# Rounded parts for both halves of the experts' down weights, with one subtraction per slot moved to GpSimd

## The chip, the core and the metric

The program runs on one core of one Trainium2 chip. The metric is the device time of one execution in microseconds (us). The core has TensorE (matrix products, PE in the rows; its weight loads are PEld), VectorE (DVE), ScalarE (ACT), GpSimd (POOL) and SyncE (SP, used here for transfers only).

## The reference, cut to what matters

Two transformer layers with attention are followed by two layers of another block. Each of these two ends in a mixture of experts:

```python
def hier_moe(h, w_rg, b_rg, w_re, b_re, w_gate, w_up, w_down):
    ...  # a gate for each of 16 experts; two experts of one group of four get one
    a = jnp.einsum('nd,edf->nef', hf, w_gate)     # d = 1024, f = 256
    b = jnp.einsum('nd,edf->nef', hf, w_up)
    hid = jax.nn.silu(a) * b * gates.astype(h.dtype)[..., None]
    return jnp.einsum('nef,efd->nd', hid, w_down).reshape(shp)
```

Everything is float32. The first mixture has 512 rows, the second 256. The change is in the last product, `hid` by `w_down`, where each expert has a weight of 256 x 1024.

## The kernel before

**Products in parts.** TensorE takes float32 operands at full precision, or operands rounded to a shorter form (fp32r) at a faster pace. For most products the kernel makes of each operand a high part, which is the rounded value, and a low part, which is the rest. It then adds three products: high by high, low by high, high by low. ScalarE makes the high parts (an activation `Copy` into an fp32r tile), VectorE the low parts (`tensor_tensor` with `subtract`, raw minus high).

**Slots.** Routing sorts the rows of a mixture by group of experts into tiles of 128 rows. A tile is worked on by the four experts of its group, one after the other. One expert on one tile is a slot `s`. The first mixture has 7 tiles and 28 slots, the second 5 tiles and 20 slots, 48 in all. Slots from 16 on take their weights by an index (`DMA_INDIRECT`, issued by GpSimd), the others by plain transfers that SyncE issues. A text that says "slot 0 to 3 of a group" means `s % 4`.

**What a slot does** (`moe` in each engine's program):

- TensorE, `gates_and_ups(s)`: 24 products of 128x512, with the transposes of the previous slot's hidden values (`turn_hidden(s - 1)`) after the 13th. Where `s % 4 == 1`, `turn_rows` follows with 8 transposes for the next tile. Then comes `downs(s - 1)`.
- ScalarE: tanh of slot `s` (L1765), in slot 1 of a group `ht_hi` (L1748), the rounding of the gate and up weights of slot `s + 2` (L1463), in slot 0 of a group the copy of a finished tile (L1755), the rounding of half of the down weight of slot `s` (L1458), and two copies of the turned hidden values (L1778, L1779).
- VectorE: two operations that finish the hidden values (L2433, L2436), in slot 1 of a group `ht_lo` (L2420), four subtractions of 128x1024 for gate and up of slot `s + 2` (`gu_lo`, L1981), one for the down weight (`dn_lo`, L1975), and `ut_lo` (L2445).
- GpSimd: gathers of rows (L2645) and of weights by index (L2650), no arithmetic within the slots.

**The down product.** The 256 rows of the weight are two halves of 128. `dn_raw[:, at, 0]` is the first half and is multiplied in full float32 with `ut_all`. `dn_raw[:, at, 1]` is the second half and goes in three products of rounded parts. Buffers for the down weight (`at = s % 2`) are two. The tile's sum over four slots stays in PSUM banks 5 and 6.

**Order.** Each engine has one program written out by hand, and waits stand in it as semaphore values. An instruction that waits holds up everything behind it on its engine. GpSimd's loop over slots first gathers rows where due, then the down weight of `s + 1` by index, then gate and up weights of `s + 4`, each once its buffer is free. The slots that gather gate and up weights are 12 to 23 of the first mixture and 12 to 15 of the second.

Of the kernel before, what the change touches and what calls it, by code (L numbers as in the profile page):

```python
# [7 lines left out]
F32 = mybir.dt.float32  # L8
# [346 lines left out]
def build(nc, a, out):  # L355
    with ExitStack() as ctx:
# [36 lines left out]
        v_tok, _ = sb("v_tok", [P, 1280])  # L393
# [9 lines left out]
        dn_raw, _ = sb("dn_raw", [P, 2, 2, D], F32, offset=acc_at)  # L403
        h_all = [sb("h_all0", [P, DT, S2], F32, offset=big2)[0], sb("h_all1", [P, DT, S], F32, offset=big2)[0]]
# [291 lines left out]
        def tensor_program(e):  # L696
# [416 lines left out]
            def moe(layer):  # L1113
# [100 lines left out]
                def downs(s):  # L1214
                    at_, first, last = s % 2, s % IN_GROUP == 0, s % IN_GROUP == IN_GROUP - 1
                    if first:
                        claim(5)
                        claim(6)
                    e.wait_ge(*(in_down_over if s >= N_EXP else in_down)[at_].at(layer, s))
                    e.wait_ge(*copied.at("ut", layer, s))  # L1220
                    for c in range(2):
                        mm(psum[:, 5 + c, :], ut_all[:, at_, :], dn_raw[:, at_, 0, c * 512:(c + 1) * 512], first, False)
                    e.wait_ge(*w_rounded.at("d", layer, s))
                    e.wait_ge(*rounded.at("ut", layer, s))
                    for c in range(2):
                        mm(psum[:, 5 + c, :], ut_hi[:, at_, :], dn_hi[:, at_, c * 512:(c + 1) * 512], False, False)
                    e.wait_ge(*rest.at("ut", layer, s))
                    for c in range(2):
                        mm(psum[:, 5 + c, :], ut_lo[:, at_, :], dn_hi[:, at_, c * 512:(c + 1) * 512], False, False)
                    e.wait_ge(*w_rest.at("d", layer, s, 1))  # L1230
                    for c in range(2):
                        d = mm(psum[:, 5 + c, :], ut_hi[:, at_, :], dn_lo[:, at_, c * 512:(c + 1) * 512], False, last)
                    d.then_inc(*multiplied.on("d", layer, s))
                    freed[5] = freed[6] = [(copied, ("y", layer, s // IN_GROUP))]
# [187 lines left out]
        def scalar_program(e):  # L1422
# [29 lines left out]
            def round_expert(kind, layer, s):  # L1452

                if kind == "d":
                    e.wait_ge(*(in_down_over if s >= N_EXP else in_down)[s % 2].at(layer, s))
                    if s >= 2:
                        e.wait_ge(*multiplied.at("d", layer, s - 2))
                    e.activation(dn_hi[:, s % 2, :], dn_raw[:, s % 2, 1, :], ACT.Copy).then_inc(  # L1458
                        *w_rounded.on("d", layer, s))
                    return  # L1460
                p = place_of[kind, layer, s]
                e.wait_ge(*(in_raw_over if s >= N_EXP else in_raw)[p % RAW_SLOTS].at(p, "all"))
                e.activation(gate_up(0, s, kind == "u"),  # L1463
                             raw[:, p % RAW_SLOTS, :].rearrange("p (k c) -> p k c", c=UC), ACT.Copy).then_inc(
                    *w_rounded.on(kind, layer, s))
# [255 lines left out]
            def moe(layer):  # L1721
# [40 lines left out]
                for s in range(slots):  # L1762
# [138 lines left out]
        def vector_program(e):  # L1901
# [510 lines left out]
            def moe(layer):  # L2412
# [16 lines left out]
                for s in range(slots):  # L2429
# [10 lines left out]
                    if s + 2 < slots:  # L2440
# [4 lines left out]
                    e.tensor_tensor(ut_lo[:, s % 2, :], psum[:, 4, P:2 * P], plain(ut_hi[:, s % 2, :]),  # L2445
                                    ALU.subtract).then_inc(*rest.on("ut", layer, s))
# [89 lines left out]
        def pool_program(e):  # L2536
# [95 lines left out]
            def moe(layer):  # L2632
# [27 lines left out]
                e.wait_ge(*routed.at("over", layer))  # L2660
                for s in range(slots):
                    t = s // IN_GROUP
                    if s % IN_GROUP == 0 and t + 3 < TILES[layer]:
                        e.wait_ge(*turned.at("row", layer, t))
                        gather_rows(t + 3)
# [4 lines left out]
                    for kind in ("g", "u"):  # L2670
                        if N_EXP <= s + 4 < slots:
# [3 lines left out]
                            gather_weights(kind, s + 4, raw[:, p % RAW_SLOTS, :], in_raw_over[p % RAW_SLOTS], p, "all")  # L2675
                for t in (TILES[layer] - 2, TILES[layer] - 1):
# [86 lines left out]
```

## Time and profile before

| | |
|---|---|
| time, median of 3 runs | 1636.26 us (1632.52 to 1637.2) |
| profiled execution, its own time | 1636.77 us |
| its span in the trace | 1635.0 us |
| PE busy | 1532.5 us (94%) |
| DVE busy | 1233.5 us (75%) |
| ACT busy | 836.5 us (51%) |
| POOL busy | 212.3 us (13%) |
| data moved | 409.12 MB, mean 250 GB/s |

A busy share is a mean over the whole program. The slots of the first mixture lie at 950 to 1198 us, those of the second at 1439 to 1614 us. A duration in a row is from an instruction's start to its end; instructions of one engine can overlap a little, so what an engine spends on one is better read from the distance between starts.

### The profile page before, as it was taken

The page shows a single profiled execution, that of the slowest core. Times are in us where ns is not written, and L with a number is a line of the kernel's source. Part 1 is how long each engine was busy: PE and PEld are TensorE (multiplying, and loading weights), DVE is VectorE, ACT ScalarE, POOL GpSimd, SP SyncE. Part 2 cuts the span into 40 slices and gives each one's busy share as a digit, 9 for nine tenths or more (in the row PEclk, how much of TensorE's full clock was granted, in tenths as well). Part 3 has the DMA queues.
Part 4 walks back from the last instruction along what each step waited for, and adds up shares of the span by engine and source line. Part 5 has one row for each costly group of instructions (what it writes and reads, how often), then busy time and mean ns, then how long its engine had stood idle before and what let it go on. Part 6 is the DMA issues. An engine that isn't in the chain of part 4 may idle for free.

```text
span 1635.0 us, 24236 instructions
## 1 busy us (share of the span) xinstructions
PE 1532.5 (94%) x9886; PEld 1290.1 (79%) x9886; DVE 1233.5 (75%) x1857; ACT 836.5 (51%) x1164; POOL 212.3 (13%) x185
## 2 busy tenths in 40 slices
PE   3899989999999998999999999999989878899998
PEld 2889888999988986899998577777767746577775
DVE  5868798888887865799986587878757784387773
ACT  2537536444543752544545556666524465456661
POOL 5050000000005000000002300033210400300020
PEclk9999999999999999999999999999988989999999
DMA  9854497999955437687881489999964631489983
GB/s 325 275 157 131 155 322 266 332 312 321 324 186 161 147 125 273 219 283 269 299 305 63 162 337 371 374 354 364 367 218 144 218 128 60 157 341 368 356 326 116
DMA packets 184926, 409.12 MB, mean 250 GB/s; under 512 B 7576, under 2 KB 136016, under 8 KB 166256
## 3 DMA queue, kind: packets, MB, share of 16 engines
q1 hardware_dynamic: 170688, 334.53, 58.2%
q0 software_dynamic: 11200, 63.49, 10.8%
q10 hardware_dynamic: 2928, 9.57, 1.5%
q8 instruction: 78, 1.28, 0.3%
q14 instruction: 32, 0.26, 0.0%
HBM read 397.07 MB, written 10.49 MB: 249 GB/s over the span
## 4 chain that ended last, share of the span: by engine, by line
PE 76%; DVE 13%; ACT 5%; DMA 4%; issue 2%; POOL 0%; SPq 0%; ACTq 0%; DVEq 0%; POOLq 0%
PE psum L704 73%; DVE acc L1969 4%; DVE w_lo L1946 3%; DMA raw<-in_w_ada 1%; ACT w_hi L1449 1%; DMA raw<-in_w_down 1%; ACT att_room L1879 1%; DVE tmp L2002 1%; PE psum L1177 1%; PE psum L1210 1%; DVE h_lo L2011 1%; DVE tmp L2183 1%; DVE stats L2514 1%; PE psum L966 1%; DMA h_rows<-tmp 1%
## 5 line engine op out<-in xcount | busy, mean ns | idle before, releaser
L1946 DVE TENSOR_TENSOR w_lo<-raw,w_hi 128x1024 fp32r<-128x1024 f32 x250 | 304.5, 1260 | 72.9 <-ACT w_hi L1449 72.8
L704 PE MATMUL psum<-h_lo,w_hi 128*128 128x256 f32 (+1 forms) x1280 | 340.0, 289 | 0.0
L704 PE MATMUL psum<-h_hi,w_lo 128*128 128x256 f32 (+1 forms) x1280 | 339.8, 289 | 0.2 <-DVE w_lo L1946 0.2
L1449 ACT ACTIVATE w_hi<-raw 128x2048 fp32r<-128x2048 f32 x125 | 238.7, 1911 | 97.7 <-DMA raw<-in_w_up 43.5
L704 PE MATMUL psum<-h_hi,w_hi 128*128 128x256 f32 (+1 forms) x1280 | 263.6, 298 | 9.3 <-DVE tmp L2183 5.7
L1969 DVE SCALAR_TENSOR_TENSOR acc<-raw,cond,acc 128x1024 f32<-128x1024 f32 x196 | 258.4, 1326 | 10.7 <-DMA raw<-in_w_ada 6.2
L704 PEld LDWEIGHTS psum<-h_hi,w_lo 128*128 128x128 f32 x1280 | 249.3, 195 | 2.0 <-DVE w_lo L1946 0.7
L704 PEld LDWEIGHTS psum<-h_lo,w_hi 128*128 128x128 f32 x1280 | 249.5, 195 | 1.4
L1981 DVE TENSOR_TENSOR gu_lo<-raw,gu_hi 128x1024 fp32r<-128x1024 f32 x184 | 213.2, 1221 | 33.5 <-ACT gu_hi L1463 33.5
L704 PEld LDWEIGHTS psum<-h_hi,w_hi 128*128 128x128 f32 x1280 | 199.5, 196 | 32.8 <-issue 18.1
L1463 ACT ACTIVATE gu_hi<-raw 128x2048 fp32r<-128x2048 f32 x96 | 178.1, 1905 | 0.0
L704 PE MATMUL psum<-gu_hi,ht_lo 128*128 128x512 f32 x384 | 151.3, 394 | 0.5 <-DVE ht_lo L2420 0.5
L704 PE MATMUL psum<-gu_lo,ht_hi 128*128 128x512 f32 x384 | 151.6, 395 | 0.0
L704 PE MATMUL psum<-gu_hi,ht_hi 128*128 128x512 f32 x384 | 148.3, 406 | 2.3 <-issue 2.3
L704 PE MATMUL psum<-u_hi,w_lo 128*128 128x256 f32 x448 | 119.0, 283 | 0.0
L704 PE MATMUL psum<-u_lo,w_hi 128*128 128x256 f32 x448 | 119.0, 283 | 0.0
L704 PE MATMUL psum<-u_hi,w_hi 128*128 128x256 f32 x448 | 99.0, 286 | 0.0
L2543 POOL TENSOR_TENSOR tmp<-tmp 128x256 f32<-128x256 f32 (+1 forms) x28 | 29.1, 1041 | 494.1 <-ACT tmp L1474 494.1
L704 PE MATMUL psum<-dn_raw,ut_all 128*128 128x512 f32 x192 | 90.3, 592 | 1.2 <-ACT ut_all L1778 1.2
L704 PEld LDWEIGHTS psum<-gu_hi,ht_hi 128*128 128x128 f32 x384 | 73.2, 191 | 16.5 <-issue 2.6
L704 PEld LDWEIGHTS psum<-u_hi,w_lo 128*128 128x128 f32 x448 | 85.9, 192 | 0.0
L704 PEld LDWEIGHTS psum<-u_lo,w_hi 128*128 128x128 f32 x448 | 85.9, 192 | 0.0
(265 smaller groups left out, 2573.6 us busy)
## 6 DMA issues: line engine op xcount, KB each, us to landing
raw<-in_w_ada SPq DMA_DIRECT2D x48, 1024.0 KB, 6.9
raw<-in_w_mod SPq DMA_DIRECT2D x48, 1024.0 KB, 6.1
raw<-in_w_in SPq DMA_DIRECT2D x34, 1024.0 KB, 5.8
raw<-in_w_up SPq DMA_DIRECT2D x32, 1024.0 KB, 5.8
raw<-in_w_down SPq DMA_DIRECT2D x32, 1024.0 KB, 6.2
raw<-in_moe_wg SPq DMA_DIRECT2D x32, 1024.0 KB, 7.5
raw<-in_moe_wu SPq DMA_DIRECT2D x32, 1024.0 KB, 7.9
dn_raw<-in_moe_wd SPq DMA_DIRECT2D x32, 1024.0 KB, 7.2
```

Source lines behind the costliest of these rows:

```text
L704: return e.matmul(o, lhs, rhs, start=start, stop=stop, skip_group_check=True)
L966: d = e.transpose(psum[:, b, j * P:(j + 1) * P], tbuf(h % 4)[:, first:first + P], ident)
L1177: d = e.transpose(psum[:, k // 4, k % 4 * P:(k % 4 + 1) * P], h_row[:, t % 3, k:D:DT], ident)
L1210: d = e.transpose(psum[:, 4, k * P:(k + 1) * P], tmp[:, s % 2, k:2 * P:2], ident)
L1449: e.activation(flat_unit(w_hi[:, split_slot(u)]), raw[:, slot, :], ACT.Copy).then_inc(*w_rounded.on(u))
L1463: e.activation(gate_up(0, s, kind == "u"), raw[:, p % RAW_SLOTS, :].rearrange("p (k c) -> p k c", c=UC), ACT.Copy).then_inc(*w_rounded.on( ...
L1879: e.activation(att_room[:, h % 4, qt * S2:(qt + 1) * S2], psum[:, 2 * (h % 2) + qt, :], ACT.Exp, bias=st[:, 2 + qt:3 + qt], scale=scale[:, ...
L1946: e.tensor_tensor(flat_unit(w_lo[:, split_slot(u), k]), raw[:, slot, part], plain(flat_unit(w_hi[:, split_slot(u), k])), ALU.subtract).the ...
L1969: e.scalar_tensor_tensor(out=a_buf, in0=src[:, k, :], scalar=s, in1=a_buf, op0=ALU.mult, op1=ALU.add).then_inc(*mod_v.on(p, n, k))
L1981: e.tensor_tensor(gate_up(1, s, kind == "u")[:, k], src[:, k], plain(gate_up(0, s, kind == "u")[:, k]), ALU.subtract).then_inc(*w_rest.on( ...
L2002: e.scalar_tensor_tensor(out=tmp[:, t % 4, c], in0=x[:, t, c], scalar=gain_col(row, chunk + 1, t), in1=psum[:, 5, c], op0=ALU.mult, op1=AL ...
L2543: e.tensor_tensor(o, o, tbuf(4 + (t + 1) % 4, n), ALU.add).then_inc(*pooled.on("sq", stage, t))
```

## The change

Both halves of the down weight are now used in rounded parts. ScalarE rounds the second half into `dn_hi` as before, and then the first half into `dn_high0` (one buffer lies where `v_tok` was, the other where `ut_all` was). VectorE still makes the second half's low part. GpSimd makes the first half's low part and writes it over the raw weights. `ut_all` is gone: `ut_hi` and `ut_lo` are now 256 wide, one copy each.

```diff
+        dn_low0, _ = sb("dn_low0", [P, 2, 2, D], F32R, offset=acc_at)
+        dn_high0 = [sb("dn_high0a", [P, D], F32R, offset=v_tok_at)[0],
+                    sb("dn_high0b", [P, D], F32R, offset=tmp_at + 2 * 2048)[0]]
...
 def downs(s):                                              # TensorE
-                    e.wait_ge(*(in_down_over if s >= N_EXP else in_down)[at_].at(layer, s))
-                    e.wait_ge(*copied.at("ut", layer, s))
-                    for c in range(2):
-                        mm(psum[:, 5 + c, :], ut_all[:, at_, :], dn_raw[:, at_, 0, c * 512:(c + 1) * 512], first, False)
-                    e.wait_ge(*w_rounded.at("d", layer, s))
+                    highs = (dn_high0[at_], dn_hi[:, at_, :])
+                    lows = (dn_low0[:, at_, 0, :], dn_lo[:, at_, :])
                     e.wait_ge(*rounded.at("ut", layer, s))
-                    for c in range(2):
-                        mm(psum[:, 5 + c, :], ut_hi[:, at_, :], dn_hi[:, at_, c * 512:(c + 1) * 512], False, False)
+                    for k in (1, 0):
+                        e.wait_ge(*w_rounded.at("d", layer, s, k))
+                        for c in range(2):
+                            mm(psum[:, 5 + c, :], ut_hi[:, at_, k, :], highs[k][:, c * 512:(c + 1) * 512],
+                               first and k == 1, False)
                     e.wait_ge(*rest.at("ut", layer, s))
-                    for c in range(2):
-                        mm(psum[:, 5 + c, :], ut_lo[:, at_, :], dn_hi[:, at_, c * 512:(c + 1) * 512], False, False)
+                    for k in (1, 0):
+                        for c in range(2):
+                            mm(psum[:, 5 + c, :], ut_lo[:, at_, k, :], highs[k][:, c * 512:(c + 1) * 512], False, False)
                     e.wait_ge(*w_rest.at("d", layer, s, 1))
                     for c in range(2):
-                        d = mm(psum[:, 5 + c, :], ut_hi[:, at_, :], dn_lo[:, at_, c * 512:(c + 1) * 512], False, last)
+                        mm(psum[:, 5 + c, :], ut_hi[:, at_, 1, :], lows[1][:, c * 512:(c + 1) * 512], False, False)
+                    e.wait_ge(*pooled.at("down_lo", layer, s))
+                    for c in range(2):
+                        d = mm(psum[:, 5 + c, :], ut_hi[:, at_, 0, :], lows[0][:, c * 512:(c + 1) * 512], False, last)
...
 round_expert("d", ...)                                     # ScalarE
-                    e.activation(dn_hi[:, s % 2, :], dn_raw[:, s % 2, 1, :], ACT.Copy).then_inc(
-                        *w_rounded.on("d", layer, s))
+                    for k in (1, 0):
+                        e.activation(dn_hi[:, s % 2, :] if k else dn_high0[s % 2][:], dn_raw[:, s % 2, k, :],
+                                     ACT.Copy).then_inc(*w_rounded.on("d", layer, s, k))
...
-                    e.activation(ut_all[:, s % 2, :], psum[:, 4, 0:P], ACT.Copy).then_inc(*copied.on("ut", layer, s))
-                    e.activation(ut_hi[:, s % 2, :], psum[:, 4, P:2 * P], ACT.Copy).then_inc(
-                        *rounded.on("ut", layer, s))
+                    e.activation(ut_hi[:, s % 2], psum[:, 4, 0:2 * P].rearrange("p (k c) -> p k c", c=P), ACT.Copy
+                                 ).then_inc(*rounded.on("ut", layer, s))
...
 vector program                                             # VectorE: ut_lo
-                    e.tensor_tensor(ut_lo[:, s % 2, :], psum[:, 4, P:2 * P], plain(ut_hi[:, s % 2, :]),
-                                    ALU.subtract).then_inc(*rest.on("ut", layer, s))
+                    e.tensor_tensor(ut_lo[:, s % 2], psum[:, 4, 0:2 * P].rearrange("p (k c) -> p k c", c=P),
+                                    plain(ut_hi[:, s % 2]), ALU.subtract).then_inc(*rest.on("ut", layer, s))
...
 pool program, moe                                          # GpSimd
+                def low_down(s):
+                    e.wait_ge(*w_rounded.at("d", layer, s, 0))
+                    e.tensor_tensor(dn_low0[:, s % 2, 0, :], dn_raw[:, s % 2, 0, :], plain(dn_high0[s % 2][:]),
+                                    ALU.subtract).then_inc(*pooled.on("down_lo", layer, s))
+
                 for s in range(slots):
                     t = s // IN_GROUP
+                    if s:
+                        low_down(s - 1)
...
+                low_down(slots - 1)
```

On TensorE, at the first down product behind a `turn_rows` in the first mixture, the order before was (the last column is the shape of the operand that moves):

```order
L1177 MATMUL psum<-cst,h_row 128x128 x8
L704 MATMUL psum<-dn_raw,ut_all 128x512 x2
L704 MATMUL psum<-dn_hi,ut_hi 128x512 x2
L704 MATMUL psum<-dn_hi,ut_lo 128x512 x2
L704 MATMUL psum<-dn_lo,ut_hi 128x512 x2
L704 MATMUL psum<-gu_hi_75,ht_hi 128x512 x2
```

and it is now:

```order
L1179 MATMUL psum<-cst,h_row 128x128 x8
L706 MATMUL psum<-dn_hi,ut_hi 128x512 x2
L706 MATMUL psum<-dn_high0a,ut_hi 128x512 x2
L706 MATMUL psum<-dn_hi,ut_lo 128x512 x2
L706 MATMUL psum<-dn_high0a,ut_lo 128x512 x2
L706 MATMUL psum<-dn_lo,ut_hi 128x512 x2
L706 MATMUL psum<-dn_low_82,ut_hi 128x512 x2
L706 MATMUL psum<-gu_hi_75,ht_hi 128x512 x2
```

The two full products on the raw half are gone and three pairs of rounded ones are there; the pair with GpSimd's low part is last.

On GpSimd, in the first mixture from slot 14 on, where the gathers of the down weight begin, the order before was:

```order
L2650 DMA raw<-in_moe_wg,over_at 128x2048
L2650 DMA raw<-in_moe_wu,over_at 128x2048
L2650 DMA dn_raw<-in_moe_wd,over_at 128x2048
L2650 DMA raw<-in_moe_wg,over_at 128x2048
L2650 DMA raw<-in_moe_wu,over_at 128x2048
L2650 DMA dn_raw<-in_moe_wd,over_at 128x2048
```

and it is now:

```order
L2657 DMA raw<-in_moe_wg,over_at 128x2048
L2657 DMA raw<-in_moe_wu,over_at 128x2048
L2670 TENSOR_TENSOR dn_low_82<-dn_raw,dn_high0a 128x1024
L2657 DMA dn_raw<-in_moe_wd,over_at 128x2048
L2657 DMA raw<-in_moe_wg,over_at 128x2048
L2657 DMA raw<-in_moe_wu,over_at 128x2048
L2670 TENSOR_TENSOR dn_low_82<-dn_raw,dn_high0b 128x1024
```

The subtraction for a slot stands behind that slot's gathers of gate and up weights.

## Rows read from the trace of the kernel before

**Rows 1.** Window: length, busy PE, PEld, DVE, ACT, POOL, PE clock, DMA share, GB/s.

```profile
1000.00:1040.00 40.00, 40.00 (x167) 29.82 (x166) 31.13 (x39) 25.83 (x29) 0.94 (x1) 1.00 0.98 384
```

**Rows 2.** Timeline, down product of slot 6 on TensorE: start, duration, engine, line, operation.

```profile
1010.09 1.88 PE L704 MATMUL psum<-dn_raw,ut_all 128*128 128x512 f32 x4
...
1012.03 0.42 PEld L704 LDWEIGHTS psum<-dn_hi,ut_lo 128*128 128x128 f32 x2
1012.50 0.42 PEld L704 LDWEIGHTS psum<-dn_lo,ut_hi 128*128 128x128 f32 x2
...
1013.19 0.62 PE L704 MATMUL psum<-gu_hi,ht_hi 128*128 128x512 f32 x2
```

**Rows 3.** Timeline of ACT: tanh of slots 0, 1, 5, 7; down rounding of 5, 7, 8.

```profile
949.80 0.38 ACT L1765 ACTIVATE tmp<-psum 128x256 f32<-128x256 f32 x1 [9.21 <-PE psum L704]
...
955.46 0.39 ACT L1765 ACTIVATE tmp<-psum 128x256 f32<-128x256 f32 x1 [0.39 <-PE psum L704]
...
991.72 0.39 ACT L1765 ACTIVATE tmp<-psum 128x256 f32<-128x256 f32 x1 [2.09 <-PE psum L704]
997.13 1.05 ACT L1458 ACTIVATE dn_hi<-dn_raw 128x1024 fp32r<-128x1024 f32 x1
...
1010.28 0.38 ACT L1765 ACTIVATE tmp<-psum 128x256 f32<-128x256 f32 x1 [2.08 <-PE psum L704]
1014.17 1.05 ACT L1458 ACTIVATE dn_hi<-dn_raw 128x1024 fp32r<-128x1024 f32 x1
...
1024.43 1.06 ACT L1458 ACTIVATE dn_hi<-dn_raw 128x1024 fp32r<-128x1024 f32 x1 [0.40 <-ACT y_row L1755]
```

**Rows 4.** Timeline of DVE, slot 7, and first the extra operation of slot 5.

```profile
993.66 1.23 DVE L2420 TENSOR_TENSOR ht_lo<-psum,ht_hi 128x1024 fp32r<-128x1024 f32 x1 [0.59 <-ACT ht_hi L1748]
...
1010.70 0.42 DVE L2433 SCALAR_TENSOR_TENSOR tmp<-tmp,psum 128x256 f32<-128x256 f32 x1 [1.07 <-ACT tmp L1765]
...
1012.50 4.63 DVE L1981 TENSOR_TENSOR gu_lo<-raw,gu_hi 128x1024 fp32r<-128x1024 f32 x4 [0.86 <-ACT gu_hi L1463]
1017.05 1.22 DVE L1975 TENSOR_TENSOR dn_lo<-dn_raw,dn_hi 128x1024 fp32r<-128x1024 f32 x1
1018.18 0.28 DVE L2445 TENSOR_TENSOR ut_lo<-psum,ut_hi 128x128 fp32r<-128x128 f32 x1
```

**Rows 5.** Line of GpSimd's own subtraction: ns min/median/max, first and last start.

```profile
L2640 POOL TENSOR_TENSOR gu_lo<-raw,gu_hi x8: 2342/2354/2367, 907.4 to 1410.3; 128x1024 fp32r<-128x1024 f32 x8
```

**Rows 6.** Timeline of POOL and DVE at 92 to 98 us, in layer one's projections.

```profile
92.53 2.20 POOL L2558 TENSOR_TENSOR qk<-tmp 128x512 f32<-128x512 f32 x1 [0.90 <-DVE tmp L2036]
97.04 1.27 POOL L2558 TENSOR_TENSOR qk<-tmp 128x512 f32<-128x512 f32 x1
...
92.36 1.22 DVE L1946 TENSOR_TENSOR w_lo<-raw,w_hi 128x1024 fp32r<-128x1024 f32 x1
...
93.50 2.32 DVE L1946 TENSOR_TENSOR w_lo<-raw,w_hi 128x1024 fp32r<-128x1024 f32 x1
```

**Rows 7.** Timeline of slots 17 and 18: tanh, and the last gather of each.

```profile
1100.48 0.39 ACT L1765 ACTIVATE tmp<-psum 128x256 f32<-128x256 f32 x1 [2.09 <-PE psum L704]
...
1109.63 1.17 POOL L2650 DMA_INDIRECT raw<-in_moe_wu,over_at  x1 [1.09 <-DVE gu_lo L1981]
...
1110.20 0.38 ACT L1765 ACTIVATE tmp<-psum 128x256 f32<-128x256 f32 x1 [2.08 <-PE psum L704]
...
1117.84 1.18 POOL L2650 DMA_INDIRECT raw<-in_moe_wu,over_at  x1 [1.10 <-DVE gu_lo L1981]
```

**Rows 8.** Windows with gaps on PE, columns as in rows 1.

```profile
64.00:68.00 4.00, 2.64 (x22) 2.43 (x21) 3.95 (x4) 3.97 (x6) 0.00 (x0) 1.00 0.53 155
68.00:72.00 4.00, 3.54 (x20) 3.25 (x21) 3.83 (x5) 4.00 (x7) 0.00 (x0) 0.59 1.07 386
72.00:76.00 4.00, 4.00 (x23) 4.00 (x22) 3.76 (x5) 1.26 (x1) 0.00 (x0) 0.56 1.06 365
452.00:456.00 4.00, 2.17 (x8) 0.90 (x6) 1.86 (x3) 0.94 (x3) 0.72 (x1) 1.00 0.96 303
```

More of the change, by code:

```diff
@@ L392, in build @@
         ctx_in, _ = sb("ctx_in", [P, 2, D], F32, offset=big1 + 16384)
-        v_tok, _ = sb("v_tok", [P, 1280])
+        v_tok, v_tok_at = sb("v_tok", [P, 1280])
         acc, acc_at = sb("acc", [P, ACCS, D])
@@ L416, in build @@
         y_tok, _ = sb("y_tok", [P, 4, D], F32, offset=big2)
-        ut_all, _ = sb("ut_all", [P, 2, P], F32, offset=tmp_at + 2 * 2048)
-        ut_hi, _ = sb("ut_hi", [P, 2, P], F32R, offset=tmp_at + 6 * 2048)
-        ut_lo, _ = sb("ut_lo", [P, 2, P], F32R, offset=tmp_at + 7 * 2048)
+        ut_hi, _ = sb("ut_hi", [P, 2, 2, P], F32R, offset=tmp_at + 6 * 2048)
+        ut_lo, _ = sb("ut_lo", [P, 2, 2, P], F32R, offset=tmp_at + 7 * 2048)
         row_at, _ = sb("row_at", [P, 4], I32)
@@ L1972, in split_expert @@
             def split_expert(kind, layer, s):
-                e.wait_ge(*w_rounded.at(kind, layer, s))
                 if kind == "d":
+                    e.wait_ge(*w_rounded.at("d", layer, s, 1))
                     e.tensor_tensor(dn_lo[:, s % 2, :], dn_raw[:, s % 2, 1, :], plain(dn_hi[:, s % 2, :]),
@@ L1977, in split_expert @@
                     return
+                e.wait_ge(*w_rounded.at(kind, layer, s))
                 src = raw[:, ring_of[kind, layer, s], :].rearrange("p (k c) -> p k c", c=UC)
```

## The prediction

> **What bounds the kernel now.** I read the windows first. In 1000 to 1040 us, inside the first mixture, TensorE is busy for all 40.00 us at a granted clock of 1.00 (2.4 GHz), VectorE for 31.13, ScalarE for 25.83, GpSimd for 0.94 [rows 1]. TensorE sets the pace and VectorE is next, with a fifth to spare. Then I read the timelines as a timetable of one slot, each time counted from the start of that slot's tanh, to see whose result comes last at the down product.
>
> *Period.* From the tanh of slot 5 to that of slot 17 are three groups of four: 1100.48 - 991.72 = 108.76, or 36.25 us a group [rows 3, 7]. Slot 17, with `turn_rows` behind it, takes 1110.20 - 1100.48 = 9.72, so the other three take (36.25 - 9.72) / 3 = 8.84 each, and `turn_rows` costs 0.88.
>
> *TensorE.* From the first matmul of a down product (1010.09) to the first one behind it (1013.19) are 3.10 us. Two loads apart by a pair of rounded matmuls are 1012.50 - 1012.03 = 0.47 apart, which makes 0.23 each [rows 2]. Six take 1.38, so the two full float32 products (four passes) take 1.72. The rest of a slot, gate, up and the turn, is 8.84 - 3.10 = 5.74. A down product begins 0.19 before the tanh of the slot after it (1010.09, 1010.28 [rows 2, 3]).
>
> *ScalarE.* The down weight is rounded from +3.89 in slot 7, from +5.41 in slot 5, and, behind the copy of the tile, from +5.3 in slot 8 (1024.43, tanh at 1010.28 + 8.84) [rows 3].
>
> *VectorE.* In slot 7 `gu_lo` (four of them, 1.14 apart) runs from +2.22, `dn_lo` from +6.77, `ut_lo` from +7.90 to +8.18. Its only idle times are 1.07 and 0.86 [rows 4], so its work is 8.84 - 1.93 = 6.91. In slot 1 of a group `ht_lo` comes on top (1.15 where the engine has more behind it) and everything after it is 1.52 later, as on ScalarE.
>
> **The change part by part.** The sum is against the profiled execution, 1636.77 us (span 1635.0 and 1.8 around it); the median of the runs is 0.5 lower.
>
> *1. TensorE, gain.* Two full products go, six rounded ones come: 1.72 - 1.38 = 0.34 a slot, 48 slots, -16.3. A down product is now 12 x 0.23 = 2.76, a plain slot 8.50.
>
> *2. ScalarE, hidden.* One more rounding (1.0 from start to start), while one wide copy replaces two. The first half's high part is there at +5.9 in slots 2 and 3, at +7.3 in slot 0, at +7.4 in slot 1. `ut_hi` follows by +6.4 or +7.9, and TensorE needs it at 8.50 - 0.19 = +8.3, or 9.38 - 0.19 = +9.2 in slot 1. ScalarE waits 2.08 before each tanh now [rows 3]. If that cover went, each slot would pay about 1.
>
> *3. VectorE, `ut_lo` twice as wide.* Like the 128x256 operation with PSUM input, 0.42 for 0.28 [rows 4]: work 7.05.
>
> *4. GpSimd's subtraction, loss.* It takes 2.35 [rows 5]. That row has no VectorE operation with two SBUF inputs beside it. Around 92 us there are some: GpSimd's `qk` takes 2.20 for 1.27 because it waits for the `w_lo` that is running, and the next `w_lo`, issued right behind the first, takes 2.32 for 1.22 because it waits for GpSimd [rows 6]. The two engines take turns, instruction by instruction. A GpSimd operation of 1.27 holds VectorE up by 1.10, so one of 2.36 does by 2.36 - 0.17 = 2.2. From below the price is nothing (GpSimd meets VectorE idle or reading PSUM), from above 2.36 and one wait more. I take 2.2, the nearest row, since `gu_lo` and `dn_lo` are the same operation as `w_lo`.
>
> [...]
>
> Where does GpSimd ask? In slots 2 and 3 at +5.9, while the third or last `gu_lo` runs. It gets the next turn, and VectorE's remaining subtractions and `ut_lo` behind them are 2.2 late. In slot 0 of a group it asks at +7.3, in `dn_lo`; behind that come only `ut_lo`, the hidden values and `ht_lo`, all with an input from PSUM, so nothing is blocked. In slot 1 it asks at +7.4, in the last `gu_lo`.
>
> TensorE waits for `ut_lo` after four matmuls of the down product now, before `dn_lo`:
> - Slot 1 of a group: `dn_lo` would start at 6.77 + 1.52 = +8.29; with the block, `ut_lo` ends at 8.29 + 2.2 + 1.13 + 0.42 = +12.05. TensorE wants it at 9.38 - 0.19 + 0.92 = +10.11. It waits 1.9.
> - Slots 2 and 3: VectorE is late already and never rests. Its turn is 7.05 + 2.2 = 9.25, about 9.2 with the overlap of neighbours, against TensorE's 8.50.
> - From the end of `ut_lo(s)` to tanh(s + 2) are 0.05 + 8 x 0.23 + 5.74 + 0.19 = 7.82. A group takes 12.05 + 2 x 9.2 + 7.82 = 38.27, against 36.25: **+2.0**, its saving of 1.4 included.
>
> The first group of a mixture has no tile to copy in slot 0, so slot 0 is blocked too: `ut_lo` ends at 6.77 + 2.2 + 1.13 + 0.42 = +10.5. VectorE then works through to slot 3: 10.5 + 3 x 9.2 + 1.15 = 39.25, and tanh(5) comes at 47.1. Before it came at 991.72 - 949.80 = 41.92 [rows 3]: **+5.1**.
>
> *5. The queue on GpSimd.* In the slots that gather gate and up weights (12 to 23, and 12 to 15), the subtraction of a slot stands behind its gathers. The last gather waits for VectorE's last `gu_lo`, and ends at 9.15 + 1.17 = +10.32 in slot 17, and at 7.64 + 1.18 = +8.82 in slot 18 [rows 7]. There is no `gu_lo` left to block, and the transfers start as before. But the low part is late: +10.32 + 2.36 + 0.1 = +12.78, wanted at 9.38 - 0.19 + 10 x 0.23 = +11.49, wait 1.3; and +11.28, wanted at +10.61, wait 0.67. The wait of slot 1 covers slot 2, `turn_rows` covers slot 0, so a group pays 1.3 + 0.67 - 1.36 = **+0.6**.
>
> *6. The last group* (slots 24 to 27, 16 to 19): slot 1 is blocked as in 4, the others have no `gu_lo` behind: 1.9 - 1.36 = +0.6, and +0.3, an estimate, for the last slot, whose second rounding and low part have little to hide behind.
>
> | | first mixture | second mixture |
> |---|---|---|
> | to slot 5 | 5.1 | 5.1 |
> | two groups at 2.0 | 4.0 | 4.0 |
> | gathering groups at 0.6 | 1.8 (three) | 0.6 (one) |
> | last group and end | 0.9 | 0.9 |
> | sum | 11.8 | 10.6 |
>
> Together +22.4: 1636.77 + 22.4 = 1659.2, or 1658.7 from the median. I predict **1659**. Blocked slots are 0 to 3, 5 to 7, 9 to 11 and the slot 1 of the last group, 11 a mixture. With 0.4 either way on each of the 22, the likeliest case's own range is 1650 to 1668.
>
> **The rivals.**
>
> *A. GpSimd doesn't hold VectorE up here, faster.* If GpSimd's turn came only after VectorE's run of subtractions, it would start at +7.9 and end at +10.3, before the +10.6 at which it is wanted. Then only the saving and parts 5 and 6 remain: -16.3 + 4 x 1.97 + 0.6 = -7.8, 1629. Against it: in rows 6 GpSimd came in between two `w_lo` that were issued back to back. For it: one place, and another GpSimd line. It also asks more of the transfers: 384 GB/s at a share of 0.98 [rows 1], times 36.25 / 34.9, is 399.
>
> *B. The transfers are the bound, no change.* If 384 GB/s is the most that the queues give, A's gain is taken back and the time stays at about 1637. Against it: ScalarE's rounding waits for no transfer in these rows.
>
> *C. The clock falls in the new gaps, slower still.* Slots 0, 5, 9 and the slot 1 of the last group leave TensorE without work for 1.9 to 3.2 us. Behind a window with 2.64 of 4 us busy the granted clock was 0.59 and 0.56 for 8 us [rows 8], which costs 8 x 0.425 = 3.4. VectorE sets the pace just then, so two slots behind at 0.7 absorb 1.4 of it, and all of it after slot 0. That leaves 2.0 + 2.0 + 3.4 a mixture, +14.8: 1674. Against it: a window with 2.17 busy at 452 us kept 1.00 [rows 8].
>
> **How the numbers follow.** The forecast has 0.62, A 0.13, B 0.06, C 0.19. This kernel's measurement tells about 0.3% (5 us) from no change. Slower: the forecast but for a sliver, and C, 0.80. Same: B and a weak form of the forecast, 0.06. Faster: A, 0.14. The range of 8 in 10 is 1637 to 1676: it leaves out A and the tail of C.
>
> **What would show it right or wrong.** Right: single `gu_lo` or `dn_lo` of about 3.4 beside a GpSimd subtraction that itself takes over 2.4; TensorE waiting for `ut_lo` by 1.9 in slots 5 and 9 and 0.7 in slots 6, 7, 10, 11; periods of 38.3 a group there and 36.9 in the gathering groups; matmuls on the first half at 0.23. Wrong: VectorE's subtractions at 1.22 throughout (A), waits of TensorE on GpSimd in slots that gather nothing, waits of ScalarE for down weights (B), or a granted clock under 0.9 within the slots (C). If GpSimd's subtraction took much more than 2.4 with nothing beside it, part 4 would be mis-sized.

## The result, and the profile after

| | before | after |
|---|---|---|
| median | 1636.73 us (1632.52 to 1637.2, 4 runs) | 1660.27 us (1658.33 to 1663.52, 4 runs) |
| profiled execution | 1636.77 us | 1663.52 us |
| first slot's tanh to the last `y_row`, first / second mixture | 248.29 / 175.47 | 262.66 / 187.73 |

The ratio is 1.0159 [1.0142, 1.0175]: slower, as predicted, and 1.3 us from the forecast of 1659. The two mixtures account for 14.4 + 12.3 = 26.6 of the 26.75 us between the two profiled executions; outside them the differences sum to 0.1 (the first mixture begins 1.3 later, and 1.2 of it is gone by the second). Of all runs reported here one showed a mean clock of 0.56 and took 2486.7 us (experiment 7's kernel); it is left out of that kernel's figures.

The window inside the first mixture, after (columns as in [rows 1]):

```profile
1000.00:1040.00 40.00, 37.18 (x168) 29.95 (x167) 36.63 (x34) 28.46 (x28) 14.12 (x5) 1.00 0.95 367
```

Against [rows 1], TensorE has 2.8 us without work, VectorE's busy time is up from 31.13 to 36.63 although it issues fewer instructions in that window (34, and 39 before), and GpSimd's is up from 0.94 to 14.12. The clock is at 2.4 GHz in both. VectorE's busy time grows by 5.5 us, and the wider `ut_lo` explains only 0.14 a slot of it: the rest is waiting inside instructions, as the next rows show.

The waits of TensorE in the first mixture, after (what it waited for; us in total, times, the longest); before, it had none on VectorE:

```profile
PE psum L706 <- DVE ut_lo L2452: 11.4, 9, 3.0
PE psum L706 <- POOL dn_low L2670: 4.9, 8, 1.2
PE psum L706 <- ACT ut_hi L1785: 0.6, 1, 0.6
```

The same lines, each with its count and shortest, median and longest duration in ns:

```profile
L1988 DVE TENSOR_TENSOR gu_lo<-raw,gu_hi x184: 1210/1219/3428, 943.1 to 1621.7; 128x1024 fp32r<-128x1024 f32 x184
...
L1981 DVE TENSOR_TENSOR dn_lo<-dn_raw,dn_hi x48: 1210/1219/3424, 957.9 to 1635.9; 128x1024 fp32r<-128x1024 f32 x48
...
L2670 POOL TENSOR_TENSOR dn_low<-dn_raw,dn_high0a x24: 2397/2840/3248, 957.0 to 1630.0; 128x1024 fp32r<-128x1024 f32 x24
```

Median and shortest of VectorE's subtractions are 1.22 and 1.21 us, as in [rows 4]; the longest is 3.42 us. The hold-up falls on a few instructions and on those it is 3.42 - 1.22 = 2.2 us. From the page's list of the costliest groups (busy us, mean ns):

```profile
L1988 DVE TENSOR_TENSOR gu_lo<-raw,gu_hi 128x1024 fp32r<-128x1024 f32 x184 | 233.1, 1328 | 21.8 <-ACT gu_hi L1470 21.8
...
L1981 DVE TENSOR_TENSOR dn_lo<-dn_raw,dn_hi 128x1024 fp32r<-128x1024 f32 x48 | 91.4, 1903 | 1.9 <-ACT dn_hi L1465 1.9
```

(1328 - 1219) x 184 = 20.1 us and (1903 - 1219) x 48 = 32.8 us, together 52.9. The single instructions show what it is made of: 22 take 3.39 to 3.43 us (15 `dn_lo` and 7 `gu_lo`), which is the number of blocked slots that the prediction had counted, and in those slots. Four more `gu_lo`, one in each gathering group, take about 2.26.

Slots 4 to 7 of after, the counterpart of [rows 4]: GpSimd's subtractions, VectorE, and TensorE's matmuls with `ut_lo` (start, duration, operation):

```profile
996.06 1.22 DVE L1981 TENSOR_TENSOR dn_lo<-dn_raw,dn_hi 128x1024 fp32r<-128x1024 f32 x1
996.68 2.84 POOL L2670 TENSOR_TENSOR dn_low<-dn_raw,dn_high0a 128x1024 fp32r<-128x1024 f32 x1 [5.76 <-ACT dn_high0a L1465]
997.20 0.42 DVE L2452 TENSOR_TENSOR ut_lo<-psum,ut_hi 128x256 fp32r<-128x256 f32 x1
...
1002.11 4.63 DVE L1988 TENSOR_TENSOR gu_lo<-raw,gu_hi 128x1024 fp32r<-128x1024 f32 x4 [0.58 <-ACT gu_hi L1470]
1005.85 3.14 POOL L2670 TENSOR_TENSOR dn_low<-dn_raw,dn_high0b 128x1024 fp32r<-128x1024 f32 x1 [6.32 <-ACT dn_high0b L1465]
1006.66 3.41 DVE L1981 TENSOR_TENSOR dn_lo<-dn_raw,dn_hi 128x1024 fp32r<-128x1024 f32 x1
1010.00 0.41 DVE L2452 TENSOR_TENSOR ut_lo<-psum,ut_hi 128x256 fp32r<-128x256 f32 x1
1010.46 0.72 PE L706 MATMUL psum<-dn_hi,ut_lo 128*128 128x512 f32 x2 [1.88 <-DVE ut_lo L2452]
1011.03 0.63 PE L706 MATMUL psum<-dn_high0b,ut_lo 128*128 128x512 f32 x2
1011.17 6.83 DVE L1988 TENSOR_TENSOR gu_lo<-raw,gu_hi 128x1024 fp32r<-128x1024 f32 x4
1011.50 0.62 PE L706 MATMUL psum<-dn_lo,ut_hi 128*128 128x512 f32 x2
1011.95 0.62 PE L706 MATMUL psum<-dn_low,ut_hi 128*128 128x512 f32 x2
1013.67 3.24 POOL L2670 TENSOR_TENSOR dn_low<-dn_raw,dn_high0a 128x1024 fp32r<-128x1024 f32 x1 [4.68 <-ACT dn_high0a L1465]
...
1019.52 0.74 PE L706 MATMUL psum<-dn_hi,ut_lo 128*128 128x512 f32 x2 [0.32 <-DVE ut_lo L2452]
```

Read them as turns. At 1005.85 GpSimd is ready while the last `gu_lo` of slot 5 runs, so its instruction is 3.14 us long: the 2.4 of work plus a wait for that `gu_lo`. VectorE issues `dn_lo` at 1006.66 and it ends only at 1010.07, a good microsecond after GpSimd at 1008.99. `ut_lo` stands behind it, and TensorE, with nothing else to do, waits 1.88 us for it. In slot 6 GpSimd comes in the middle of the four `gu_lo`, which take 6.83 us for the 4.63 of [rows 4]. In slot 4, at the top, GpSimd starts beside a `dn_lo`, and what follows on VectorE reads PSUM: `ut_lo` keeps its 0.42 while GpSimd is working.

The tanh of slots 5, 6, 7 and 9, the counterpart of [rows 3]:

```profile
998.36 0.39 ACT L1772 ACTIVATE tmp<-psum 128x256 f32<-128x256 f32 x1 [1.48 <-PE psum L706]
...
1007.72 0.38 ACT L1772 ACTIVATE tmp<-psum 128x256 f32<-128x256 f32 x1 [1.67 <-PE psum L706]
...
1018.34 0.38 ACT L1772 ACTIVATE tmp<-psum 128x256 f32<-128x256 f32 x1 [2.14 <-PE psum L706]
...
1036.81 0.39 ACT L1772 ACTIVATE tmp<-psum 128x256 f32<-128x256 f32 x1 [1.79 <-PE psum L706]
```

A group now takes 1036.81 - 998.36 = 38.45 us, where [rows 3, 7] gave 36.25.

### The profile page after: what moved, and what is told of

It is laid out like the page before. It is cut to its first block, busy times and chain, and to the rows that moved or that the text cites. A ratio compares the mean times of both kernels' runs of the same rounds, so it can differ in the third digit from the quotient of the medians.

```text
span 1661.7 us, 24428 instructions
## 1 busy us (share of the span) xinstructions
PE 1528.3 (92%) x9982; PEld 1310.1 (79%) x9982; DVE 1290.5 (78%) x1857; ACT 877.8 (53%) x1164; POOL 360.4 (22%) x233
## 4 chain that ended last, share of the span: by engine, by line
PE 61%; DVE 23%; ACT 7%; DMA 3%; POOL 3%; issue 2%; SPq 0%; ACTq 0%; DVEq 0%; POOLq 0%
PE psum L706 59%; DVE gu_lo L1988 6%; DVE acc L1975 4%; DVE dn_lo L1981 3%; DVE w_lo L1952 3%; ACT gu_hi L1470 2%; DMA raw<-in_w_ada 1%; POOL dn_low L2670 1%; ACT att_room L1885 1%; ACT w_hi L1455 1%; POOL raw L2657 1%; DVE tmp L2009 1%; DVE h_lo L2018 1%; PE psum L1179 1%; DVE tmp L2190 1%
## 5 line engine op out<-in xcount | busy, mean ns | idle before, releaser
L1975 DVE SCALAR_TENSOR_TENSOR acc<-raw,cond,acc 128x1024 f32<-128x1024 f32 x196 | 258.3, 1325 | 10.6 <-DMA raw<-in_w_ada 6.1
L1988 DVE TENSOR_TENSOR gu_lo<-raw,gu_hi 128x1024 fp32r<-128x1024 f32 x184 | 233.1, 1328 | 21.8 <-ACT gu_hi L1470 21.8
L1981 DVE TENSOR_TENSOR dn_lo<-dn_raw,dn_hi 128x1024 fp32r<-128x1024 f32 x48 | 91.4, 1903 | 1.9 <-ACT dn_hi L1465 1.9
L2670 POOL TENSOR_TENSOR dn_low<-dn_raw,dn_high0a 128x1024 fp32r<-128x1024 f32 x24 | 66.8, 2782 | 98.0 <-ACT dn_high0a L1465 97.7
```

The source lines that it names most:

```text
L1975: e.scalar_tensor_tensor(out=a_buf, in0=src[:, k, :], scalar=s, in1=a_buf, op0=ALU.mult, op1=ALU.add).then_inc(*mod_v.on(p, n, k))
L1988: e.tensor_tensor(gate_up(1, s, kind == "u")[:, k], src[:, k], plain(gate_up(0, s, kind == "u")[:, k]), ALU.subtract).then_inc(*w_rest.on( ...
L2670: e.tensor_tensor(dn_low0[:, s % 2, 0, :], dn_raw[:, s % 2, 0, :], plain(dn_high0[s % 2][:]), ALU.subtract).then_inc(*pooled.on("down_lo", ...
```

## The experiments

Two theories stood against each other at the start. The first: GpSimd's subtraction holds VectorE's subtractions up, and TensorE waits for what stands behind them. Its rival: the work itself is too long for its place (more rounding, a later `ut_hi`, a low part that is late), and the hold-up is covered. Each kernel ran on one chip beside the kernel before, whose median there was 1634.84 us for experiments 1 to 4, 1635.03 for 5 and 6, and 1634.18 for 7 and the second run of 4's kernel. "Kernel 1" is the kernel of experiment 1, and so on.

**1. Without GpSimd's subtraction.** The last pair of the down product takes `dn_lo` again, so the first half's low part is left out of the result; the number of matmuls stays.

```
-    e.wait_ge(*pooled.at("down_lo", layer, s))
-        d = mm(..., ut_hi[:, at_, 0, :], lows[0][...], False, last)
+        d = mm(..., ut_hi[:, at_, 0, :], lows[1][...], False, last)
-    def low_down(s): ...        (and its calls)
```

> The changed kernel without GpSimd's subtraction; the last pair of matmuls takes VectorE's low part of the second half again, so the first half's low part is left out of the result. All matmuls and ScalarE's second rounding stay. Theory L (GpSimd's read of SBUF holds VectorE up, and its queue makes the low part late in the gathering slots): all that the change costs is gone and the saving of TensorE stays, 48 x 0.34 = 16 us, so 1620 to 1623, with no wait of TensorE for ut_lo. Rival S (ScalarE's extra rounding and the wide copies delay the chain): 1650 or more, the waits for ut_lo stay. Rival M (six rounded matmuls are no faster than two full ones): 1636.

Measured: 1621.61 us (1618.95 to 1625.2), ratio 0.9924 [0.9904, 0.9945]. By the ratios the subtraction costs 1.0159 - 0.9924 = 2.35%, or 38 us, and everything else in the change gains 13 (1634.8 - 1621.6). A plain slot takes 8.43 us here, against 8.84 before. The extra rounding and the wider `ut_lo` are still in this kernel, so they aren't what made the changed one slower. They aren't free either: 0.41 a slot would be 19.7 us over 48 slots, and 13 arrived. In the first mixture TensorE waits 0.80 us for `ut_lo` in slot 0, and 2.74 for `ut_hi` in the last slot, behind the two roundings of a down weight that lands late. From slot 0 to slot 5 are 41.57 us (41.92 before), and the last group takes 27.2 (25.1 before).

**2. The subtraction at a place where it meets few two-input subtractions.** GpSimd waits for VectorE's `dn_lo` of the slot as well. The same work, moved.

```
 def low_down(s):
     e.wait_ge(*w_rounded.at("d", layer, s, 0))
+    e.wait_ge(*w_rest.at("d", layer, s, 1))
```

> The changed kernel with one more wait: GpSimd's subtraction starts only when VectorE's dn_lo of the same slot is done, so that only VectorE operations with an input from PSUM are beside it. Nothing else is changed. Theory L: no gu_lo or dn_lo takes more than 1.3 us in the plain slots; TensorE waits about 0.35 for the low part in slot 1 of a group, so a plain group is 1.0 shorter than before the change; the gathering groups stay as they are now (37.3 us, 1.05 longer than before). Sum about 1630 to 1634. Rival S, or a rival by which GpSimd's operation is simply too slow: a later start can't help, 1660 or more.

Measured: 1637.69 us (1634.44 to 1640.39, 10 runs), ratio 1.0019 [1.0006, 1.0031]. The hold-up is nearly gone: the longest `gu_lo` is 2.26 instead of 3.43, the longest `dn_lo` 1.76 instead of 3.42, and GpSimd's own instruction is its bare 2.4 us:

```profile
L1988 DVE TENSOR_TENSOR gu_lo<-raw,gu_hi x184: 1210/1218/2261, 940.6 to 1597.8; 128x1024 fp32r<-128x1024 f32 x184
...
L2671 POOL TENSOR_TENSOR dn_low<-dn_raw,dn_high0a x24: 2386/2408/2432, 956.8 to 1604.7; 128x1024 fp32r<-128x1024 f32 x24
```

I had expected no `gu_lo` over 1.3 us in the plain slots; slot 6 still has one of 1.57, because GpSimd's instruction runs into it. That one wait takes 22.6 us off. The time is 4 above the top of what I expected, and TensorE's waits in the first mixture say where most of it lies:

```profile
PE psum L706 <- POOL dn_low L2671: 6.6, 12, 1.2
...
PE psum L706 <- ACT ut_hi L1785: 1.6, 1, 1.6
PE psum L706 <- DVE ut_lo L2452: 0.8, 1, 0.8
```

The low part, begun after `dn_lo`, is itself late in slot 1 of a group (a plain group takes 1026.98 - 991.26 = 35.72, where kernel 1 has 34.69). The gathering groups stay at 1099.98 - 1062.70 = 37.28, as in the changed kernel: there the hold-up isn't what costs the time.

**3. `ut_lo` ahead of `dn_lo` on VectorE.** TensorE then doesn't wait for `ut_lo` behind a held-up `dn_lo`.

```
-    split_expert("d", layer, s)
     e.wait_ge(*rounded.at("ut", layer, s))
     e.tensor_tensor(ut_lo[...], psum[...], plain(ut_hi[...]), ALU.subtract)...
+    split_expert("d", layer, s)
```

> The changed kernel with VectorE's ut_lo ahead of its dn_lo. GpSimd's turn now falls together with ut_lo, which reads PSUM. Theory L: the waits of TensorE for ut_lo vanish, VectorE's turn in a blocked slot is 8.85 instead of 9.2, and a group of plain slots takes about 36.2, as before the change; the first group of a mixture costs 2.8 more, the gathering groups 1.05. Sum about 1642 to 1650. A rival by which only the place of ut_lo behind dn_lo is at fault (and not what GpSimd takes from VectorE): the full saving, 1625 or less. Rival S: 1660.

Measured: 1654.67 us (1651.63 to 1655.57), ratio 1.0113 [1.0094, 1.0132], nearly 5 above the top of my range. A plain group falls from 38.45 only to 1032.08 - 995.22 = 36.86, and a gathering one rises from 37.3 to 1107.22 - 1068.94 = 38.28. TensorE's waits move to what now comes last:

```profile
PE psum L706 <- POOL dn_low L2670: 6.7, 10, 1.2
PE psum L706 <- DVE dn_lo L1981: 4.8, 5, 1.7
```

So an order helps only by the slack between two uses: the held-up time is still in VectorE's turn. A gathering slot becomes longer than in the changed kernel (9.96, 9.73 and 9.30 for slots 13, 14 and 15), and the trace shows where: from one gather of a down weight on GpSimd to the next are 1139.87 - 1130.61 = 9.26 us, against 9.00 in the changed kernel, and in between the gather of the up weight takes 1.22 instead of 0.94. What makes that gather longer I did not settle.

**4. VectorE makes both low parts.** GpSimd does no arithmetic; VectorE subtracts in the order `dn_lo`, `ut_lo`, `dn_low`.

```
+    e.wait_ge(*w_rounded.at("d", layer, s, 0))
+    e.tensor_tensor(dn_low0[...], dn_raw[...], plain(dn_high0[...]), ALU.subtract
+                    ).then_inc(*w_rest.on("d", layer, s, 0))
-    e.wait_ge(*pooled.at("down_lo", layer, s))
+    e.wait_ge(*w_rest.at("d", layer, s, 0))
-    def low_down(s): ...        (and its calls)
```

> The changed kernel with the first half's low part made by VectorE too, behind ut_lo, and no arithmetic on GpSimd within the slots. VectorE's work per slot is 7.05 + 1.13 = 8.2 against TensorE's 8.5, and 9.35 against 9.38 in slot 1 of a group. Theory L: VectorE's operation costs it 1.13 where GpSimd's cost it 2.2, and no queue is in the way: 1620 to 1624, the full saving of 16 us, faster than both kernels. A rival by which VectorE has no room for any more work: 1636 or more, with TensorE waiting for ut_lo or the low part in slots 1 to 3.

Measured: 1625.46 us (1623.2 to 1627.09), ratio 0.9936 [0.9918, 0.9954], 1.5 above the top of my range. The full computation, faster than both kernels. A window inside the first mixture (columns as in [rows 1]), and slot 6 on VectorE:

```profile
1000.00:1040.00 40.00, 40.00 (x185) 33.26 (x184) 38.60 (x44) 30.57 (x31) 0.94 (x1) 1.00 1.00 397
...
1004.39 4.63 DVE L1988 TENSOR_TENSOR gu_lo<-raw,gu_hi 128x1024 fp32r<-128x1024 f32 x4
```

and the new line, all 24 of one buffer:

```profile
L2455 DVE TENSOR_TENSOR dn_low<-dn_raw,dn_high0a x24: 1209/1214/1217, 958.7 to 1596.3; 128x1024 fp32r<-128x1024 f32 x24
```

Every one takes 1.21 us. TensorE never rests in that window although VectorE is busy for 38.60 of the 40 us. A plain group is 1027.30 - 992.64 = 34.66. VectorE's extra 1.13 a slot (start to start) is half of the 2.2 for which GpSimd's help held it up. The same kernel once more, beside kernel 7:

> The kernel of e_dve once more, beside e_last. Theory L: the saving of TensorE is 0.41 a slot by e_dve's own timeline (8.43 for 8.84), 19.7 in all; ten microseconds of it are to be seen as 0.6% in the time, 1623 to 1627.

Measured: 1623.9 us (1619.67 to 1628.53), the same ratio 0.9936 [0.9917, 0.9955].

**5. The kernel before, with the subtraction alone.** To see the hold-up without the changed matmuls, the old kernel gets a GpSimd subtraction of the same size and place, into a tile that is not read by anything; the last pair of the down product waits for it. It is ready one rounding earlier than in the change and falls into VectorE's run of subtractions more often: 28 of them take over 3.3 us here, 22 in the changed kernel.

```
+    def low_down(s):
+        e.wait_ge(*w_rounded.at("d", layer, s))
+        ...
+        e.tensor_tensor(spare[:], dn_raw[:, s % 2, 1, :], plain(dn_hi[:, s % 2, :]),
+                        ALU.subtract).then_inc(*pooled.on("down_lo", layer, s))
```

> The kernel before the change, all its matmuls, ScalarE and VectorE operations kept, with one operation more: in each slot GpSimd subtracts dn_hi from the raw second half into a spare tile (128x1024, two inputs in SBUF, as in the change), and TensorE's last pair of the down product waits for it. The result is not touched. Theory L: GpSimd asks at +5 in slots 1 to 3 and at +6.3 in slot 0 of a group, always within VectorE's run of subtractions, so VectorE's turn is 9.0 against TensorE's 8.84 and a plain group takes 37.2 instead of 36.25; the first group of a mixture pays 3.5, the gathering groups 0.5. Sum 1645 to 1650. If GpSimd's operation takes nothing from VectorE, the time stays at 1635.

Measured: 1646.71 us (1644.3 to 1650.98), ratio 1.0069 [1.0045, 1.0093]. The first group goes from 41.92 to 997.29 - 952.03 = 45.26, a plain one from 36.25 to 1034.15 - 997.29 = 36.86.

```profile
L1983 DVE TENSOR_TENSOR gu_lo<-raw,gu_hi x184: 1210/1219/3437, 944.0 to 1609.1; 128x1024 fp32r<-128x1024 f32 x184
...
PE psum L705 <- DVE ut_lo L2447: 2.8, 3, 1.7
PE psum L705 <- POOL spare L2667: 1.7, 3, 0.6
```

With nothing else changed the same long subtractions and the same wait of TensorE for `ut_lo` appear. The wait is smaller, since TensorE's own slot of 8.84 hides more of VectorE's turn. The gathering groups take 37.3 here too (36.25 before), where I had expected 36.75.

**6. The queue on GpSimd.** As kernel 2, but in the gathering slots (12 to 23, and 12 to 15) VectorE makes the low part.

```
+    if 12 <= s < slots - 4:
+        ...tensor_tensor(dn_low0[...], ..., ALU.subtract)    (on VectorE)
-    if s:
+    if s and not 12 <= s - 1 < slots - 4:
         low_down(s - 1)
```

> As e_wait (GpSimd's subtraction waits for dn_lo), but in the gathering slots (12 to 23 and 12 to 15) VectorE makes the first half's low part, so that no subtraction stands behind gathers on GpSimd. Theory Q (what e_wait still pays is GpSimd's queue of gathers in front of the subtraction): those four groups fall from 37.3 to 34.7 us each, 10.5 in all, 1626 to 1629. If the queue has no part in it, 1637 as e_wait.

Measured: 1628.78 us (1624.92 to 1633.83, 10 runs), ratio 0.9969 [0.9952, 0.9987]. The gathering groups fall from 37.3 to 1095.10 - 1060.41 = 34.69, the plain ones stay at 35.72. That is 8.9 us off kernel 2, all from four groups (4 x 2.6 = 10.4, of which 2.5 are lost at the end of the first mixture).

**7. The last slot.** In kernel 4 the last slot of the first mixture takes over 10 us, in part because ScalarE rounds the late down weight before it copies `ut_hi`. Here the copy comes first, in that slot alone, and `ut_lo` ahead of the low parts.

```
-    round_expert("d", layer, s)
+    if s < slots - 1:
+        round_expert("d", layer, s)
     e.activation(ut_hi[...], psum[...], ACT.Copy)...
+    if s == slots - 1:
+        round_expert("d", layer, s)
```

> e_dve, and in the last slot of each mixture ScalarE copies ut_hi before it rounds the down weight, and VectorE makes ut_lo first. In e_dve TensorE waited 2.7 us for ut_hi there in the first mixture, since the gathered weight comes late and two roundings stood in front, and its clock fell behind the gap. Theory: the first matmuls start about 1.3 earlier (the wait 1.4), the last slot of the first mixture takes 8 to 9.5 instead of 10.3, the time is 1 to 2 us below e_dve's, which the timing can hardly tell. If the late weight alone sets the end, the last slot stays at 10.3.

Measured: 1623.08 us (1622.69 to 1629.48, 5 runs), ratio 0.9946 [0.9927, 0.9965]; kernel 4 beside it gave 1623.9. The trace shows the effect (tanh to `y_row` of the last slot 1187.31 - 1177.93 = 9.38, and 1193.68 - 1183.23 = 10.45 in kernel 4), but 1 us a mixture can't be told in the time. ScalarE in the last slot of kernel 4:

```profile
1183.23 0.38 ACT L1772 ACTIVATE tmp<-psum 128x256 f32<-128x256 f32 x1 [2.14 <-PE psum L706]
1186.71 1.06 ACT L1465 ACTIVATE dn_hi<-dn_raw 128x1024 fp32r<-128x1024 f32 x1 [3.10 <-DMA dn_raw<-in_moe_wd,over_at]
...
1188.62 0.36 ACT L1785 ACTIVATE ut_hi<-psum 128x256 fp32r<-128x256 f32 x1
```

The weight of the last slot doesn't land earlier when TensorE is faster. From the tanh of slot 25 to this rounding are 20.35 us here (1186.71 - 1166.36) and 20.38 in the kernel before (1193.35 - 1172.97), so what the last two slots save on TensorE is spent in waiting for it.

## Why the prediction was right, and where its terms were off

The direction, the size and the mechanism were right. The differences of the profiled executions beside the terms, in us:

| | forecast | first mixture | second mixture |
|---|---|---|---|
| to slot 5 | +5.1 | +5.4 | +6.7 |
| each plain group | +2.0 | +2.2, +3.8 | +2.2, +2.2 |
| each gathering group | +0.6 | +1.0, +1.1, +1.0 | +1.1 |
| last group and end | +0.9 | -0.1 | +0.1 |
| sum | 11.8 / 10.6 | 14.4 | 12.3 |

That the median came within 1.3 us of the forecast is partly luck: between the profiled executions the mixtures cost 26.6 where the terms give 22.4. Of the 4.2 more, 3 are the clock (rival C below) and 1.8 the gathering groups, and the last groups take 1.8 back.

*Step 1, TensorE's gain: mis-sized.* I took 3.10 - 2.76 = 0.34 a slot. A slot in which nothing is late takes 8.43 instead of 8.84 (kernels 1 and 4), so it is 0.41, and 19.7 for 48 slots instead of 16.3. The pairs of matmuls stand 0.47 and 0.45 apart in the rows above (1011.03, 1011.50, 1011.95). In kernel 1 a whole down product takes 1008.07 - 1005.35 = 2.72 and the rest of the slot 1013.79 - 1008.07 = 5.72: 0.04 of the other 0.07 is in the twelve matmuls, and the rest of it outside them. On the other side, kernel 1 turned only 13 of the 19.7 into time.

*Steps 2 and 3, the extra rounding and the wider `ut_lo`: held* from slot 5 on, where the plain slots of kernel 4 have all of that work and wait for nothing; not in the first slots of a mixture and in the last slot of the first, where kernel 1 shows the waits given above. That ScalarE's cover would fail there was in no term.

*Step 4, the hold-up: held.* Duration 3.42, TensorE's wait of 1.88 in slot 5 against 1.9, a plain group of 38.45 against 38.27, the first group of 47.28 against 47.1. The two slots behind slot 5 take 9.08 and 9.39 (tanh of slot 7 to that of slot 9) against 9.2 each. Kernel 5 shows the hold-up with the old matmuls, kernel 2 takes nearly all of it away. How long it lasts is 2.2 of GpSimd's 2.4 us and not all of them. With 2.2 a plain group was to be 38.27, with the 2.36 that was its upper bound 38.27 + 3 x 0.16 = 38.75; it is 38.45, or 38.43 in the second mixture. The Trainium skill (page "SBUF — State Buffer", section "Who interferes with whom") says that a VectorE instruction with two SBUF inputs contends with a GpSimd instruction that reads SBUF. The trace agrees as to which instructions are held up: 26 of VectorE's subtractions, and none of its operations with an input from PSUM.

*Step 5, the queue on GpSimd: mechanism right, too small.* I let the gathers be as fast as in [rows 7] and looked for what they delay. GpSimd in slots 18 and 19 of after:

```profile
1127.89 1.99 POOL L2657 DMA_INDIRECT dn_raw<-in_moe_wd,over_at  x1 [1.06 <-PE psum L706]
1130.18 1.96 POOL L2657 DMA_INDIRECT raw<-in_moe_wg,over_at  x1 [0.30 <-DVE gu_lo L1988]
1132.45 0.94 POOL L2657 DMA_INDIRECT raw<-in_moe_wu,over_at  x1 [0.30 <-issue]
1133.41 2.42 POOL L2670 TENSOR_TENSOR dn_low<-dn_raw,dn_high0a 128x1024 fp32r<-128x1024 f32 x1
...
1136.89 1.99 POOL L2657 DMA_INDIRECT dn_raw<-in_moe_wd,over_at  x1 [1.06 <-PE psum L706]
```

This is a closed chain of 1136.89 - 1127.89 = 9.00 us. The down weight's gather waits for the matmuls that read its buffer, the two others and the subtraction follow in order, and the last pair of the next product waits for the subtraction. The chain is longer than TensorE's 8.43, so it sets the slot. I had the low part late by 1.3 and 0.67 in two slots of a group; by the slots' lengths (9.94, 9.00 and 9.01 in the changed kernel, 8.43 where nothing is late) it is 1.5, 0.6 and 0.6 in three. Before, the subtraction was not in the chain, and kernel 6 takes it out: the groups go to 34.69. The gather of the down weight is part of it as well: it takes 1.99 here and 0.94 in most slots before, and an estimate from these rows with 0.94 gives 7.95, below 8.43. No run separates the two. The step was also wrong that there is no `gu_lo` left to block: in slot 1 of each gathering group the subtraction runs into the next slot's first `gu_lo`, which takes 2.26.

*Step 6, the last group: wrong, and small.* I added 0.9; it was nothing. The end of a mixture waits for the last gathered down weight (the rounding at 1186.71 in experiment 7's rows), and the kernel before waited for it too, which covers what the group loses. In kernels 1 and 4 the first mixture's last group even takes 27.2 against 25.1 before: TensorE waits 2.74 for `ut_hi` behind the two roundings, and the granted clock of the four microseconds behind is 0.57 and 0.59.

*Rival C, the clock, happened in part.* Windows of after (columns as in [rows 8]):

```profile
1008.00:1012.00 4.00, 2.12 (x10) 1.44 (x9) 3.96 (x5) 4.00 (x4) 0.99 (x1) 1.00 0.99 410
1048.00:1052.00 4.00, 3.09 (x9) 2.47 (x10) 3.96 (x7) 4.00 (x4) 0.00 (x0) 0.73 0.60 250
1052.00:1056.00 4.00, 4.00 (x17) 3.27 (x17) 4.00 (x2) 0.19 (x2) 3.24 (x1) 0.84 0.73 258
1464.00:1468.00 4.00, 4.00 (x10) 3.13 (x11) 3.96 (x5) 2.31 (x3) 1.62 (x1) 0.50 0.10 43
```

TensorE is without work for the same 1.88 us in slots 5 and 9. Behind the first gap the clock stays at 2.4 GHz, behind the second it falls: 0.73 over four microseconds, part of them at 1.2 GHz. That group is 1.6 longer than its neighbour (40.01 and 38.45), the other side of +3.8 against +2.2 in the table. The gap in slot 0 is 2.98 us in both mixtures and the clock falls behind both: 0.64 in the window at 960 us in the first, and 1.2 GHz for a whole window in the second, whose first group is 1.4 longer. The rival's condition is met three times in this execution (slot 0 of both mixtures, slot 9 of one). Where it shows in a group's length its price is 1.6 + 1.4 = 3 us, not the 15 that I gave it; most gaps left the clock alone.

*Rivals A and B are out.* A needs VectorE's subtractions at 1.22 throughout, and the rows show 3.42. B held the transfers to be the limit at 384 GB/s; kernel 4 runs through a plain group in 34.66 instead of 36.25, with 397 GB/s in the window shown, so there was more to be had.

The whole loss, apportioned by the runs (to a microsecond or two, since the kernel before had medians from 1634.2 to 1636.7 on the chips used): 1660.3 to 1637.7 by taking the hold-up away (22.6), to 1628.8 by taking the subtraction out of the gathers' queue (8.9), to 1623.9 or 1625.5 with VectorE doing the low part of the other slots too, and 1621.6 without the subtraction at all (in the traces of kernels 4 and 1 the two mixtures differ by 1.4 us together). What the rounded parts were worth with the full computation was 9 to 10 us (kernel 4 against the kernel before beside it); by the ratios, 1.0159 - 0.9936, GpSimd's way of helping cost 36.

## What to carry to other kernels

Arithmetic that is moved to GpSimd to spare VectorE has to be priced by what runs on VectorE at that moment: here each GpSimd subtraction that fell among VectorE's operations with two SBUF inputs cost VectorE almost its own length (2.2 us of 2.4, where VectorE does the same work in 1.13), and beside operations that read PSUM it cost nothing. Before anything is put on a queue that also issues transfers, follow that queue as a closed chain and compare its period with the period of the bounding engine. If an order or a wait is changed against a hold-up, look at what comes last then; here no move of the subtraction made the kernel as fast as giving the work back to the faster engine did.

## What the hardware showed that I had not expected

- The gathers of down weights became twice as long on GpSimd. The same line, before and then after (ns shortest/median/longest):

```profile
L2650 POOL DMA_INDIRECT dn_raw<-in_moe_wd,over_at x16: 936/937/1705, 1086.5 to 1601.6; - x16
```

```profile
L2657 POOL DMA_INDIRECT dn_raw<-in_moe_wd,over_at x16: 947/1944/1991, 1099.9 to 1629.0; - x16
```

The long rows don't need a subtraction in that queue: in kernel 4, which has none there, the gathers of down weights take 0.94 to 1.91 us. And a longer row need not end later. The gather of a gate weight right behind that of a down weight took 1.17 us after 1.09 idle before (at 1115.57) and takes 1.96 after 0.30 idle now (at 1130.18); its end is 2.25 and 2.26 us behind the end of the one ahead of it. What sets the length wasn't separated.
- The same gap of 1.88 us on TensorE comes four times in one execution, before the matmuls at 1010, 1048, 1514 and 1552 us. Only the second was followed by a lower clock. I can't tell it apart from the others by the rows.
- `ut_lo` and `ht_lo`, which read PSUM and an SBUF tile, kept 0.41 and 1.22 us in every one of their instances (409 to 425 ns and 1218 to 1225 ns), although some ran beside GpSimd's subtraction, as the `ut_lo` of slot 4 does and, for 0.48 us, the `ht_lo` at 1116.03. Whether a GpSimd operation that reads PSUM would leave VectorE's subtractions alone as well wasn't tried.
